# Border columns of the head convolutions on GpSimd, one ScalarE write for each panel, and the third convolution behind the last masks

## The reference, cut to what matters

```python
def _dwconv(x, w):                      # width 3, one zero on either side
    p = w.shape[0] // 2
    return lax.conv_general_dilated(x, w[:, None, :].astype(x.dtype), window_strides=(1,), padding=[(p, p)],
                                    dimension_numbers=('NWC', 'WIO', 'NWC'), feature_group_count=x.shape[-1])

def _dn_inputs(p, dn_conv):
    y = jax.nn.silu(_dwconv(p[6], dn_conv)).astype(jnp.float32)      # p[6] = u @ w_in + b_in, 3 x 1024 columns
    q, k, v = [t.reshape(B, T, DN_HEADS, DN_DIM) for t in jnp.split(y, 3, axis=-1)]
    return (_l2norm(q), _l2norm(k), v) + ...

# in _gated_delta_chunked, for each head and chunk of 64 tokens:
    a_mat = jnp.where(strict, jnp.einsum('nbhid,nbhjd->nbhij', kb, kc) * decay_mat, 0.0)
    sol = lax.linalg.triangular_solve(a_mat, rhs, left_side=True, lower=True, unit_diagonal=True)
```

## Time and profile before

| | |
|---|---|
| median of three runs | 2984.23 us (2984.11 to 2984.51) |
| the profiled execution | 2987.26 us, its span 2985.5 us |
| PE busy | 2935.2 us, 98% of the span |
| DVE busy | 1930.0 us, 65% |
| ACT busy | 1460.4 us, 49% |
| POOL busy | 355.5 us, 12% |
| chain that ended last | PE 90%, ACT 4%, DVE 3%, issue 2% |
| mean granted TensorE clock | 0.998 |

### The profile page before, as it was taken

How to read it: one execution, slowest core, us unless ns; L and a number is a source line. 1 busy time by engine, 2 the same in 40 slices (tenths; PEclk the granted TensorE clock), 3 DMA queues, 4 the chain that set the end, 5 groups by cost and what they waited for, 6 DMA issues and landing times.

```text
span 2985.5 us, 50450 instructions
## 1 busy us (share of the span) xinstructions
PE 2935.2 (98%) x17768; PEld 2469.1 (83%) x17768; DVE 1930.0 (65%) x3479; ACT 1460.4 (49%) x2497; POOL 355.5 (12%) x272
## 2 busy tenths in 40 slices
PE   8999999999999999999999999999999999999998
PEld 5888888888887788888888888888888889799887
DVE  5766766766535834445665766757777766766777
ACT  5222258777546732234222242223788867644654
POOL 0000024434101000000000000000244321000000
PEclk9999999999999999999999999999999999999999
DMA  7544421211221032233444534434222114155454
GB/s 289 193 169 176 169 93 50 70 57 50 78 91 66 22 99 99 99 100 113 169 155 148 183 120 162 165 138 176 79 71 70 63 61 160 44 177 176 163 183 155
DMA packets 101845, 365.63 MB, mean 122 GB/s; under 512 B 11216, under 2 KB 12880, under 8 KB 101584
## 3 DMA queue, kind: packets, MB, share of 16 engines
q1 hardware_dynamic: 98384, 353.02, 34.3%
q10 hardware_dynamic: 3328, 10.81, 1.1%
HBM read 362.67 MB, written 1.11 MB: 122 GB/s over the span
## 4 chain that ended last, share of the span: by engine, by line
PE 90%; ACT 4%; DVE 3%; issue 2%; DMA 1%; SPq 0%; DVEq 0%; ACTq 0%; POOLq 0%; POOL 0%
PE bank L2125 69%; PE bank L2104 4%; PE bank L2106 2%; PE bank L2683 1%; PE bank L2398 1%; PE bank L2423 1%; PE bank L2465 1%; PE bank L2656 1%; PE bank L2669 1%; PE bank L2395 1%; PE bank L2455 1%; PE bank L2476 1%; ACT ada_raw L946 1%; PE bank L2488 1%; PE bank L2486 1%
## 5 line engine op out<-in xcount | busy, mean ns | idle before, releaser
L584 ACT ACTIVATE whi<-raw 128x1024 fp32r<-128x1024 f32 x518 | 546.7, 1058 | 991.4 <-PE bank L2125 964.1
L2125 PE MATMUL bank<-uh,whi 128*128 128x512 f32 (+1 forms) x2688 | 1000.9, 372 | 6.2 <-DVE ul L1395 2.0
L2125 PE MATMUL bank<-uh,wlo 128*128 128x512 f32 (+1 forms) x2688 | 980.3, 365 | 0.0
L2125 PE MATMUL bank<-ul,whi 128*128 128x512 f32 (+1 forms) x2688 | 974.8, 363 | 0.0
L1312 DVE TENSOR_TENSOR wlo<-raw,whi 128x1024 fp32r<-128x1024 f32 x476 | 583.4, 1226 | 368.7 <-ACT whi L584 353.4
L2125 PEld LDWEIGHTS bank<-uh,whi 128*128 128x128 f32 x2688 | 508.3, 189 | 95.8 <-issue 23.0
L2125 PEld LDWEIGHTS bank<-uh,wlo 128*128 128x128 f32 x2688 | 508.3, 189 | 73.0 <-issue 3.4
L2125 PEld LDWEIGHTS bank<-ul,whi 128*128 128x128 f32 x2688 | 508.6, 189 | 71.2 <-issue 3.8
L2125 PE MATMUL bank<-bh,whi 128*128 128x512 f32 (+1 forms) x930 | 340.1, 366 | 0.8 <-DVE bl L2044 0.8
L2125 PE MATMUL bank<-bl,whi 128*128 128x512 f32 (+1 forms) x930 | 337.6, 363 | 0.0
L2125 PE MATMUL bank<-bh,wlo 128*128 128x512 f32 (+1 forms) x930 | 337.6, 363 | 0.0
(11 more groups left out here) (309 smaller groups left out, 3838.6 us busy)
## 6 DMA issues: line engine op xcount, KB each, us to landing
raw<-stream SPq DMA_DIRECT2D x520, 512.0 KB, 3.3
ada_raw<-stream SPq DMA_DIRECT2D x132, 512.0 KB, 4.3
gc_row<-gc_rows ACTq DMA_DIRECT2D x16, 512.0 KB, 3.7
m<-stream SPq DMA_DIRECT2D x5, 512.0 KB, 12.1
h<-h_in SPq DMA_DIRECT2D x1, 2048.0 KB, 9.8
cst<-consts SPq DMA_DIRECT2D x1, 1104.0 KB, 9.2
lmat<-stream SPq DMA_DIRECT2D x2, 512.0 KB, 11.5
gc_row<-stream SPq DMA_DIRECT2D x2, 512.0 KB, 12.0
```

The costliest lines, as they stand in the source:

```text
L584: act.activation(whi[:, j, :], raw[:, j, :], ACT.Copy).then_inc(hi_ready, 1)
L2125: last = mm(bank[j if to is None else to][:, c0:c1], w(t, a), x[:, t, c0:c1], start=n == 0, stop=n == 3 * kts - 1)
```

## The change

It has four parts.

1. `prep_tap` writes the whole panel in one ACT operation, with the full bias in the border columns too.
2. A new function `edges` on GpSimd subtracts from columns 0 and 255 of each segment the bias of the tap that isn't there (a 128x2x2 operation, for the query of layer 1 128x2). It waits for `tap_ready` and signals `edge_ready`, for which DVE's first part now waits. In `head_vectors` two subtractions go.
3. In GpSimd's steps the edges of key and query stand behind the first `split` and ahead of `masked`, and those of the value between the two `low_squares`. Those of head 0 stand ahead of the first `masked`.
4. On DVE the first part of the third convolution goes from behind the mask of place 10 to behind that of place 11, and its second part to behind the first `XT`.

```diff
@@ gpsimd, heads(l)
+                def edges(b, n):
+
+                    j = (1, 0, 2)[n]
+                    a = c0 // CTX if j == 0 else 0
+                    x = kraw[:, :] if j == 1 else qkv[:, j, :]
+                    ends = x.rearrange("p (s t) -> p s t", s=2)[:, a:2, 0:256:255]
+                    bias = hx[:, j:j + 7:6].rearrange("p (s e) -> p s e", s=1).broadcast_to([128, 2 - a, 2])
+                    pool.wait_ge(E["tap_ready"], 3 * (l * DNH + b) + n + 1)
+                    pool.tensor_tensor(ends, ends, bias, ALU.subtract).then_inc(E["edge_ready"], 1)
+
@@ gpsimd, step(b, follow, after)
                     if after:
                         split(P[("head", l)][0] + b + 2, 0)
                     if follow:
+                        edges(b + 1, 0)
+                        edges(b + 1, 1)
                         masked(o + 1)
                         if not after:
                             split(P[("head", l)][0] + b + 2, 0)
-                        for n in range(2):
-                            low_squares(b + 1, n)
+                        low_squares(b + 1, 0)
+                        edges(b + 1, 2)
+                        low_squares(b + 1, 1)
                         split(P[("head", l)][0] + b + 2, 1)
                         split(P[("head", l)][0] + b + 2, 2)
 
+                for n in range(3):
+                    edges(0, n)
                 masked(l * DNH)
@@ scalar, prep_tap
-                for lo, hi, e in ((1, CTX - 1, 9), (0, 1, 0), (CTX - 1, CTX, 6)):
-                    last = act.activation(y[:, :, lo:hi], p[:, :, lo:hi], ACT.Identity, scale=hv[:, 5 + 3 * j:6 + 3 * j],
-                                          bias=hx[:, e + j:e + j + 1])
-                last.then_inc(E["tap_ready"], 1)
+                act.activation(y, p, ACT.Identity, scale=hv[:, 5 + 3 * j:6 + 3 * j], bias=hx[:, 9 + j:10 + j]).then_inc(E["tap_ready"], 1)
@@ vector, head_vectors
-                dve.tensor_tensor(e[0], e[3], e[0], ALU.subtract)
-                steps.do(dve.tensor_tensor(e[2], e[3], e[2], ALU.subtract))
-                steps.sync()
@@ vector, prep_conv
-                    dve.wait_ge(E["tap_ready"], 3 * o + n + 1)
+                    dve.wait_ge(E["edge_ready"], 3 * o + n + 1)
@@ vector, head(l, b, follow)
-                        if follow and at in (3, 7, 10):
+                        if follow and at in (3, 7, 11):
                             prep_conv(l, b, at // 4, second=False)
-                        if follow and at in (5, 9, 11):
-                            prep_conv(l, b, at // 4 - 1 if at < 11 else 2, first=False)
+                        if follow and at in (5, 9):
+                            prep_conv(l, b, at // 4 - 1, first=False)
                 for d in range(2):
                     dve.wait_ge(E["q_sum"], 14 * o + 12 + d + 1)
                     dve.tensor_tensor(c4d(XT[:, d, :]), bc(ident, TC, 128), c4d(bank[4 + d][:, :]), ALU.subtract).then_inc(E["xt_ready"], 1)
+                    if follow and d == 0:
+                        prep_conv(l, b, 2, first=False)
```

## The result

The changed kernel takes 3030.7 us (median of four runs, 3030.47 to 3033.89) against 2984.37 us for the kernel before in the same session. The ratio is 1.0154 with a 95% interval of 1.0141 to 1.0166: 46 us slower. Forecast were 3028 us and a range of 3014 to 3046.

The account below looks back on a forecast made before the run. PE, busy 98% of the span, was taken as the bound. Waits net of gains of 27.5 us (layer 0) and 8.7 (layer 1), 2.3 for round 1 and 5 for the clock gave 43.5 us more: 3028 us, range 3014 to 3046.

Parts of the forecast that it names:

- What bounds: Whole kernel: PE is busy 98% of the span, so time is won or lost only where PE waits.
- The gains: PE's waits at level 6 go: 0.37 us a round in layer 0, 1.06 in layer 1, 10.0 us together.
- The wait behind GpSimd's queue: Level 3, twelve rounds: key's edges come late; PE waits 4.70 us in layer 0, 2.25 in layer 1.
- The clock: Clock falls at half of layer 0's six waits, none in layer 1: 5 us, bounds nothing to 20.
- The rival with falls in all twelve rounds: Clock falls in every stalled round of both layers: 20 us in place of 5, 3043 us; chance 0.14.
- Round 1: Round 1 of each layer: late value's edges delay XT, losing 0.65 us in layer 0, 1.60 in layer 1.
- The value's edges in the other rounds: Twelve shifted rounds: edges done after 5.5 us, wanted after 6.1, so nothing is lost.
- The rival: Value's edges bind in each round: at most 0.5 us in 12 rounds, 3034 us; chance 0.08.

Follow-up runs that it names:

- no_edges: Kernel before with one ScalarE write per panel and the moved value convolution, no GpSimd edges, border columns left uncorrected: 2976.16 us, ratio 0.9967.
- wait_half_filled: Changed kernel plus 9 (layer 0) or 4 (layer 1) 128x256 filler products on TensorE ahead of level 3: 3025.93 us, ratio 1.0134 to the kernel before.
- edges_in_time: Changed kernel with GpSimd's key edges behind Qt, query's behind the tail, value's ahead of the key's squares: 2980.55 us, ratio 0.9985 to the kernel before.
- edges_before_panel: Changed kernel with the key's and query's edges ahead of the first weight panel on GpSimd: 3003.77 us, ratio 1.0060 to the kernel before.
- value_edges_late: edges_in_time with the value's edges back between GpSimd's two squares, as in the changed kernel: 3001.74 us, ratio 1.0051 to the kernel before.

## Why the prediction was right

**What bounds.** Right. PE's order is fixed, and nothing made up for a wait: the time went where PE waited, round by round.

**The gains.** Right in size. 0.37 us was said for a round of layer 0 and 1.06 for one of layer 1. Alone they are 0.41 and 0.96 (no_edges), and 9 to 10 us in all. ScalarE's one write was said to cover the wait of 0.56 in layer 1, and the moved part the other. The runs of the single parts show this for layer 1 (39.00 and 38.99 us, 0.49 and 0.50 less than before). In layer 0 either would have been enough.

**The wait behind GpSimd's queue.** Right, in place, number and size. Said were 4.70 us at PE and 4.6 us net for a round of layer 0. Recorded are 4.43, and the round without falls of the clock is 4.40 us longer (wait_half_filled). In all PE waits 38.5 us for the mask, where 42 were said. In layer 1 1.45 us were said and 1.3 found (40.77 against 39.49). The operation's price was taken as 0.2 us and is 0.21. edges_in_time and edges_before_panel show the cause in two doses.

**The clock.** This term was too small, though inside its bounds: 5 us by three falls in layer 0 were said, and 9.7 us by six came. The price of one was right (1.7 us said, 1.6 found in the mean), the count was not. So the rounds of layer 0 repeat after 50.2 to 51.2 us and not after 49 to 50. That no fall comes in layer 1 was right. The rival with falls in all twelve rounds is out. The Trainium skill (TensorE: Matmul & The Clock Gate, "Why this matters for your kernels") says to leave no long idle gaps between bursts of products, or the clock goes down. The trace agrees for the waits of 4.4 us. The page speaks of longer gaps than 2.1 us, and at waits of 2.0 to 2.1 us the clock fell in three rounds of twelve over two kernels.

**Round 1.** 0.65 and 1.60 us were said, 0.3 and 1.5 found. DVE waits 2.41 us there for the value's edges in layer 1, and PE then 1.05 us for `XT`. One premise was wrong and did no harm: in step 0 the edges of the next head's key don't stand ahead of everything, but behind `Qt` and `IT`. These were done at 446.36 in layer 0, and the key's edges then waited 6.42 us for ScalarE's panel.

**The value's edges in the other rounds.** The reckoning that they don't bind while the round is shifted was right: DVE waits for them only twice, in the rounds 1. Counted from PE's start of level 3, the edges were said to be done after 5.5 us and wanted after 6.1. In wait_half_filled, where no fall of the clock stretches the round, they are done after 5.5 us (563.56 against 558.07) and wanted after 5.95. The rival is out for this kernel, but value_edges_late shows that it was held off by the first fault alone.

The sum was 43.5 us. The spans differ by 43.4 us, where too little clock (-4.7) and too much elsewhere (1.1 + 0.8 + 0.5 in the rounds and 2.4 outside) cancel. That the sum agrees to 0.1 us is therefore luck. The medians, by which the time is given, differ by 46.3 us, 2.8 more than the sum, mostly because the profiled execution of before lies 2.9 us above its median.

## What to carry to other kernels

When a correction is given to an idle engine, what counts is where it stands in that engine's queue at the moment it is wanted, and not how idle the engine is on average: GpSimd was busy for 12% and still 5.5 us late. Lay the timelines of the engine that gets the work and of the one that waits for it side by side for one round, and put the work at the first place where its input is there. When such a wait goes, look for the next one that it covered. And a wait in front of TensorE can cost more than its length, since the clock may fall with it: here 4.4 us of waiting cost 1.0 to 2.0 us more.

## What was not expected of the hardware

- Of waits of 2.14 us, which are alike in six rounds, three had a fall of the clock at or just behind their end and three had none (edges_before_panel). Waits of 1.96 to 2.03 us in layer 1 of the changed kernel had none in six. Why these differ stays open.
- A 128x256 product in float32 takes two records of 0.22 us each, where the projections' products of that size start every 0.12 us: 18 calls are 36 records and 7.9 us.
- A GpSimd operation on 128x4 takes 0.20 to 0.22 us and one on 128x2 takes 0.19 to 0.21 us, but for two of the 48 that stand ahead of the rounds (0.74 and 0.27 us). So its cost is nearly all fixed, as the fit to the earlier trace rows had it (0.18 us).
